# Turning the mLSTM's keys, values and heads by VectorE and DMA instead of TensorE; the norm's weight on the output gate

## The reference, cut to what matters

```python
s = jnp.einsum('bjhd,bshd->bhjs', q, k) * w                 # w: decay weights of a chunk
num = jnp.einsum('bhjs,bshe->bjhe', s, v) + inter * (q @ C)
h = num / jnp.maximum(jnp.abs(den), floor)
C_new = decay * C + jnp.einsum('bhs,bshd,bshe->bhde', w_last, k, v)
...
h = h * lax.rsqrt(jnp.mean(h * h, axis=-1, keepdims=True) + EPS)   # per head
h = (h.reshape(B, T, D_A) * p['mlstm_norm']).astype(x.dtype)
ya = (h * jax.nn.sigmoid(o)) @ p['w_proj_a']
```

## Time and profile before

| | |
|---|---|
| median of 3 runs | 1904.1 us (1902.83 to 1904.41) |
| span of the profiled execution | 1901.1 us |
| PE busy | 1881.8 us (99%) |
| DVE busy | 1348.0 us (71%) |
| ACT busy | 868.2 us (46%) |
| POOL busy | 110.5 us (6%) |
| DMA packets, bytes | 126553, 272.88 MB |

### The profile page before, as it was taken

The page is one execution under the profiler, slowest core; times in us unless marked ns, Lnnn a source line. Parts: engine busy times, 40 slices in busy tenths (PEclk is TensorE's granted clock), DMA queues, the critical chain, the costliest instruction groups (busy, mean ns, idle before and its releaser), DMA issues.

```text
span 1901.1 us, 33354 instructions
## 1 busy us (share of the span) xinstructions
PE 1881.8 (99%) x13291; PEld 1857.3 (98%) x13291; DVE 1348.0 (71%) x2082; ACT 868.2 (46%) x1629; POOL 110.5 (6%) x165
## 2 busy tenths in 40 slices
PE   9999999999999999999999999999999999999997
PEld 8999999999999999999999999999999999999997
DVE  7788999999987764784454378967777776746363
ACT  5554445444554455551122355644454444635342
POOL 0011111111111111110000000000000000000000
PEclk9999999999999999999999999999999999999999
DMA  3556676666657655458131333212222223556654
GB/s 135 160 142 151 163 186 162 165 184 172 188 171 199 195 157 155 145 157 338 45 139 45 119 100 104 81 69 79 81 81 69 77 83 113 183 202 210 208 172 160
DMA packets 126553, 272.88 MB, mean 144 GB/s; under 512 B 21820, under 2 KB 61500, under 8 KB 126400
## 3 DMA queue, kind: packets, MB, share of 16 engines
q1 hardware_dynamic: 111280, 235.16, 36.1%
q0 software_dynamic: 15120, 35.59, 10.3%
HBM read 206.97 MB, written 63.74 MB: 142 GB/s over the span
## 4 chain that ended last, share of the span: by engine, by line
PE 91%; DVE 4%; DMA 2%; issue 1%; ACT 1%; SPq 0%; POOL 0%; DVEq 0%; ACTq 0%; POOLq 0%
PE ps L1202 9%; PE ps L1204 9%; PE ps L1203 9%; PE ps L1367 7%; PE ps L1368 7%; PE ps L1369 7%; PE ps L1567 7%; PE ps L1565 7%; PE ps L1566 7%; PE ps L1587 4%; PE ps L1588 4%; PE ps L1589 4%; PE ps L1295 2%; PE ps L1292 1%; DMA araw<-wts 1%
## 5 line engine op out<-in xcount | busy, mean ns | idle before, releaser
L1202 PE MATMUL ps<-rx,fhi 128*128 128x364 f32 (+2 forms) x736 | 248.7, 338 | 0.1
L1203 PE MATMUL ps<-rx,fhi 128*128 128x364 f32 (+2 forms) x736 | 238.0, 323 | 0.0
L1204 PE MATMUL ps<-rx,flo 128*128 128x364 f32 (+2 forms) x736 | 238.0, 323 | 0.0
L1367 PE MATMUL ps<-rx,ahi 128*128 128x304 f32 (+1 forms) x672 | 194.4, 289 | 0.4 <-DVE v L2588 0.4
L1368 PE MATMUL ps<-rx,ahi 128*128 128x304 f32 (+1 forms) x672 | 193.7, 288 | 0.0
L1369 PE MATMUL ps<-rx,alo 128*128 128x304 f32 (+1 forms) x672 | 193.6, 288 | 0.0
L1587 PE MATMUL ps<-ghi,dhi 128*128 128x384 f32 (+1 forms) x528 | 173.2, 328 | 2.8 <-DVE glo L2949 2.0
L1588 PE MATMUL ps<-glo,dhi 128*128 128x384 f32 (+1 forms) x528 | 172.2, 326 | 0.0
L1589 PE MATMUL ps<-ghi,dlo 128*128 128x384 f32 (+1 forms) x528 | 172.2, 326 | 0.0
L2942 DVE TENSOR_TENSOR dlo<-draw,dhi 128x1408 fp32r<-128x1408 f32 x48 | 77.8, 1624 | 118.1 <-ACT dhi L2154 118.0
L1202 PEld LDWEIGHTS ps<-rx,fhi 128*128 128x128 f32 x736 | 138.6, 188 | 1.9 <-issue 0.3
(11 more groups left out here) (367 smaller groups left out, 5721.7 us busy)
## 6 DMA issues: line engine op xcount, KB each, us to landing
draw<-wdn SPq DMA_DIRECT2D x48, 704.0 KB, 4.2
araw<-wts SPq DMA_DIRECT2D x105, 256.0 KB, 3.9
uraw<-wts SPq DMA_DIRECT2D x44, 512.0 KB, 4.3
fraw<-wts SPq DMA_DIRECT2D x27, 512.0 KB, 3.8
qkv<-scr_qkv SPq DMA_DIRECT2D x22, 544.0 KB, 8.4
scr_g<-cva SPq DMA_DIRECT2D x22, 512.0 KB, 2.6
alo<-wts POOLq DMA_DIRECT2D x42, 256.0 KB, 5.1
graw<-scr_g SPq DMA_DIRECT2D x43, 192.0 KB, 4.1
```

Of the source, the lines that this page charges most:

```text
L1202: pe.matmul(b, hi[:, w], src[:, his[k], cols], start=(k == 0), stop=False)
L1203: pe.matmul(b, hi[:, w], src[:, los[k], cols], start=False, stop=False)
L1204: mm = pe.matmul(b, lo[:, w], src[:, his[k], cols], start=False, stop=(k == KB - 1))
L1367: pe.matmul(b, ahi[s][:, c], bhi[:, k, :], start=(fresh and k == 0), stop=False, skip_group_check=True)
```

## The change: what it does

- The keys and values are no longer turned by PE. SP loads the values of one chunk (`load_values`, three slots before the step) to `vin`; the keys stand in `qkv` as before, the value blocks of it are no longer loaded. DVE transposes squares of 32x32 inside both (`turn`, two slots before). SP stores the squares to a new DRAM tensor `scr_t` in such an order that the 128x128 blocks are turned (`store_turned`: four DMAs of 32 partitions each, in runs of 32 elements), and loads them back as `kvt`, keys and values side by side (`load_turned`, one DMA in rows of 128 elements). Before this load SP waits until the stores have landed and until ACT has weighted the keys of the step before.
- ACT weights the keys in place in SBUF (`weighted_keys`), one slot after the load; the copy of the values is gone.
- The head is turned by one DVE transpose of `zt` in squares (`rows_out`, DVE, two slots after the step); SP stores it in runs of 32 elements (`store_head`, four DMAs a step, two in the last chunk of each head).
- The norm's weight is put on the output gate: ACT makes mnq * tanh + mnq over the finished tile (one more operation of 1088 columns for each of the eight tiles, with a wait of SP's store on it), and `gated_head` is a plain product.
- `vin` and the two `turned` buffers lie where blocks 2 and 3 of head 0's `qkv` buffer were, so blocks 3 and 6 of the second pass change places (`C_HI`).

```diff
             def load_head(h):
...
-                for b in range(6):
+                for b in (0, 1, 4, 5):
                     sp.dma_start(qkv[h % 2][:, b, :], scr_qkv[h, b]).then_inc(qk_in, 16)
+            def load_values(i):
+                h, j = STEPS[i]
+                if i:
+                    sp.wait_ge(turned_set, 2 * i)
+                sp.dma_start(vin[:, :, :], scr_qkv[h, 2:4, :, step_cols(j)].rearrange("b p n -> p b n")).then_inc(v_part_in, 16)
+            def store_turned(i):
+                sp.wait_ge(turned_set, 2 * i + 2)
+                for a in range(4):
+                    rows = slice(32 * a, 32 * a + 32)
+                    sp.dma_start(scr_t[i][:, :, rows].rearrange("k (b n) q -> n (k b) q", n=32),
+                                 turned[i % 2][rows, :, :].rearrange("n k (b q) -> n (k b) q", q=32)).then_inc(turned_out, 16)
+            def load_turned(i):
+                if i >= 2:
+                    sp.wait_ge(n_full, i - 1)
+                if i:
+                    sp.wait_ge(kw_set, i)
+                sp.wait_ge(turned_out, 64 * (i + 1))
+                sp.dma_start(kvt[i % 2][:, 0:2 * DH]..., scr_t[i]...).then_inc(kvt_in, 16)
+            def store_head(i):
+                sp.wait_ge(zs_set, i + 1)
+                for b in Z_PARTS[i]:
+                    sp.dma_start(scr_z[2 * h:2 * h + 2, :, at + 32 * b:at + 32 * b + 32].rearrange("k (a q) n -> q (k a) n", q=32),
+                                 zs[i % 2][32 * b:32 * b + 32, :].rearrange("q (a n) -> q a n", n=32)).then_inc(z_out[i % 2], 16)
...
             for s, ((kind, k), c) in enumerate(SLOTS):          # SP
+                i = step_at(s, 0)   ->  load_turned(i)
+                i = step_at(s, -1)  ->  store_turned(i)
+                i = step_at(s, -3)  ->  load_values(i)
...
+                i = step_at(s, 3)   ->  store_head(i)
...
             def scores(i):                                       # PE
-                    pe.wait_ge(kv_copied, 2 * i)
-                for b in range(4):
-                    mm = pe.transpose(bank(2, b * P, P), q[:, b, cols], ident[:, :])
-            def rows_out(i):
-                for b in range(2):
-                    mm = pe.transpose(bank(3, 256 + b * L, L), zt[i % 2][:, b * P:(b + 1) * P], ident[:, :])
...
             def scores(i):                                       # ACT
-                act.activation(vt[p][:, 0:DH], bank(2, DH, DH), ACT.Copy).then_inc(kv_copied, 1)
-                act.activation(kw[p][:, :], bank(2, 0, DH), ACT.Copy, scale=gt[...])
+            def weighted_keys(i):                                # at step_at(s, 1), ahead of scores
+                act.wait_ge(kvt_in, 32 + 16 * (i + 1))
+                act.activation(kvt[p][:, 0:DH], kvt[p][:, 0:DH], ACT.Copy, scale=gt[...]).then_inc(kw_set, 1)
-                    act.activation(zs[p][:, b, :], bank(3, 256 + b * L, L), ACT.Copy, scale=mnq[...]).then_inc(zs_set, 1)
+                        act.activation(spl[i % 2][:, :], spl[i % 2][:, :], ACT.Identity, bias=mnq[:, k:k + 1], scale=mnq[:, k:k + 1])
...
+            def turn(i):                                         # DVE, at step_at(s, -2)
+                dve.wait_ge(turned_out, 64 * (i - 1))
+                dve.wait_ge(v_part_in, 32 + 16 * (i + 1))
+                dve.transpose(turned[p][:, 2:4, :], vin[:, :, :]).then_inc(turned_set, 1)
+                dve.transpose(turned[p][:, 0:2, :], qkv[h % 2][:, 0:2, step_cols(j)]).then_inc(turned_set, 1)
+            def rows_out(i):                                     # DVE, at step_at(s, 2), ahead of turn
+                dve.wait_ge(zt_set, i + 1)
+                dve.transpose(zs[p][:, :], zt[p][:, :]).then_inc(zs_set, 1)
...
-                dve.scalar_tensor_tensor(z, fx[:, n, :], 1.0, z, ALU.add, ALU.mult).then_inc(zo_set, 1)
+                dve.tensor_tensor(z, fx[:, n, :], z, ALU.mult).then_inc(zo_set, 1)
```

More of the change, by code:

```diff
@@ L94 @@
 SPL_OF = {"u": (0, 2), "g": (1, 2), "k": (1, 1), "v": (0, 0), "q": (0, 0)}
-SPL_AT = [1 + sum(sum(SPL_OF[kind]) for kind, _ in PAIRS_B[:i]) for i in range(NB + 1)]
+SPL_AT = [2 + sum(sum(SPL_OF[kind]) for kind, _ in PAIRS_B[:i]) for i in range(NB + 1)]
 V0_STORES = [[1 - p + len(range(p, min(i, NB), 2)) for i in range(NB + 2)] for p in range(2)]
@@ L203, in step_at, with z_stored @@
     return STEP_IN.get(NTH_FULL[s] - after)
[L206 to L213, removed]
+Z_PARTS = [range(L // 32) if j < NCHUNK else range((L - DEC) // 32, L // 32) for _, j in STEPS]
+def z_stored(i):
+    return 16 * sum(len(Z_PARTS[n]) for n in range(i % 2, i, 2))
 def step_cols(j):
@@ L463, in build @@
     qkv = [Room(at_rz + s * 6 * blk)(f"qkv{s}", [P, 6, T]) for s in range(2)]
+    room = Room(at_rz + 2 * blk)
+    vin = room("vin", [P, 2, L])
+    turned = [room(f"turned{s}", [P, 4, L]) for s in range(2)]
+    assert room.at <= at_rz + 4 * blk
     room = Room(at_rz + 6 * blk)
@@ L479, in build @@
     cb = [room(f"cb{s}", [P, 2, VW]) for s in range(2)]
-    vt = [room(f"vt{s}", [P, VW]) for s in range(2)]
-    kw = [room(f"kw{s}", [P, DH]) for s in range(2)]
+    kvt = [room(f"kvt{s}", [P, DH + VW]) for s in range(2)]
     wt = [room(f"wt{s}", [P, L]) for s in range(2)]
@@ L484, in build @@
     zt = [room(f"zt{s}", [P, DH]) for s in range(2)]
-    zs = [room(f"zs{s}", [P, 2, L]) for s in range(2)]
+    zs = [room(f"zs{s}", [P, DH]) for s in range(2)]
     nb = [room(f"nb{s}", [P, L]) for s in range(2)]
@@ L640, in build @@
         zt_set = sem("zt_set")
-        z_full = sem("z_full")
         zs_set = sem("zs_set")
@@ L861, in _ @@
             for s, ((kind, k), c) in enumerate(SLOTS):
+                i = step_at(s, 0)
+                if i is not None:
+                    load_turned(i)
+                i = step_at(s, -1)
+                if i is not None:
+                    store_turned(i)
+                i = step_at(s, -3)
+                if i is not None:
+                    load_values(i)
                 i = step_at(s, 1)
@@ L923, in _ @@
                     sp.dma_start(c_out[0][:, STEPS[i][0]], cb[0][:, :, :]).then_inc(cp_out, 16)
+                i = step_at(s, 3)
+                if i is not None:
+                    store_head(i)
                 i = step_at(s, 4)
@@ L1423, in _ @@
                     gate_turn()
-                i = step_at(s, 3)
-                if i is not None:
-                    rows_out(i)
                 i = step_at(s, 1)
@@ L1747, in evac @@
                         act.activation(spl[i % 2][:, :], spl[i % 2][:, :], ACT.Copy, bias=0.5, scale=0.5).then_inc(spl_set, 1)
+                    if kind == "o" and c == NC - 1:
+                        act.wait_ge(t_free, EVAC_AT[s])
+                        act.activation(spl[i % 2][:, :], spl[i % 2][:, :], ACT.Identity, bias=mnq[:, k:k + 1], scale=mnq[:, k:k + 1])\
+                            .then_inc(spl_set, 1)
                 elif kind == "mu":
@@ L1881, in _ @@
                     a_hi(0, 5), a_hi(0, 6), a_hi(0, 2), a_hi(0, 7), a_hi(0, 4), a_minus(0, 2), a_minus(0, 4)
+                i = step_at(s, 1)
+                if i is not None:
+                    weighted_keys(i)
                 i = step_at(s, 0)
@@ L2660, in _ @@
                     gate_columns()
+                i = step_at(s, 2)
+                if i is not None:
+                    rows_out(i)
+                i = step_at(s, -2)
+                if i is not None:
+                    turn(i)
                 i = step_at(s, 0)
```

88 lines of the change are left out of this document (42 added, 46 removed).

## The result

The changed kernel takes 1983.9 us (median of 4, 1982.3 to 1986.2), the kernel before 1903.8 us on the same chip: ratio 1.0422 (95% interval 1.0410 to 1.0435). It is 80 us slower. I forecast 1926 us with a range of 1886 to 1972: the sign was right, the size was not.

What follows compares the result with a forecast made beforehand. The prediction took the DMA engines' work to bound the steps: 292 us plus 6 us for SP's order gives 298 instead of 276, so 1901.1 + 22 + 3 = 1926 us, range 1886 to 1972.

Steps and rivals of the forecast that it cites:

- What bounds it: Stretch of all steps: PE bounds before, busy 99%; DVE and DMA get its work, and DMA was thought to decide.
- the gate: ACT's extra operation of 1.10 us on each of eight output gate tiles: costed at nothing, up to 1 us.
- TensorE, -0.65 us a step: PE loses four transposes (0.43 us) and the head's two (0.22 us) a step: 23.4 us over 36 steps.
- VectorE, 0.33 us a transpose, step of 6.6 us: DVE gains three transposes, 1.0 us a step; at 6.6 us it just keeps PE's new pace in the tap steps.
- The packets' price, 12.2 ns: Time of one 128-byte packet on one DMA engine, from a line through the 120-byte and 256-byte prices.
- rival 3: Scattered 128-byte writes cost about 24 ns, twice the small bursts' price: 1986 us, chance 0.15.
- DMA's work, 268 us, and a step of 8.1 us: DMA work in the steps' stretch rises from 160 to 268 us; with `nb`'s pauses a step takes 8.1 us, 36 make 292.
- `nb`'s quiet part: Load of `nb` occupies SP's queue 1.5 us a step, each engine busy a tenth of the time; later transfers wait.
- SP's order: SP issues 4.4 of 6.6 us a step, keeping pace if stores land under 4.35 us; later heads' blocks add 6 us.
- a share under 0.8: Sign in the profile after: late PE steps with DMA share under 0.8 mean the order of SP's list is the cause.
- a share over 0.9: Sign for the forecast in the profile after: DMA share over 0.9 in the steps' stretch, with steps 8.1 us apart.

Runs made afterwards that it cites:

- 1904.8 with nothing turned: Changed kernel without the keys' and values' DMA trip and VectorE transposes (ScalarE copies them unturned), head stored early in one transfer: 1904.8 us.
- the run where ScalarE stores and nobody reads: Changed kernel, ScalarE copies replacing the keys' and values' reload, head stored early in one transfer; ScalarE issues their four 128-byte-packet stores, read by nobody: 1932.6 us.
- the kernel with ScalarE's stores: Changed kernel with the head's store one slot earlier and the four stores of turned keys and values issued by ScalarE one slot earlier: 1939.3 us.
- 1976.4: Changed kernel with the head's store and the stores of turned keys and values each one slot earlier, all issued by SP: 1976.4 us.

## Why the prediction was right and wrong

The forecast was a stretch 22 us longer; it became 79 us longer, 16.7 before the first step and 62.7 in the steps. Put in a row, differences between runs come near the whole: 1904.8 with nothing turned, + 9.8 for VectorE's transposes, + 40.0 for the keys' and values' store, + 33.0 for the head's store narrow and late, gives 1987.6 against 1983.9 measured. This does not show that the reload and the serial trip cost nothing. The 40.0 us were measured with the stores in another place than the changed kernel has them, the 33.0 us with two alterations at once and without the trip, while the head's early store gives back only 20 in the changed kernel. That the sum fits may be luck.

- **What bounds it.** Right in that the loss lies with VectorE and DMA, which got the work, and that the gate costs nothing (1903.5 us). Wrong in what of DMA it is: not the engines' work, but issuing and landing in SP's queue.
- **TensorE, -0.65 us a step.** Right for the head's 0.22 us, which the head part alone gives back in full. For the 0.43 us of keys and values it is not shown.
- **VectorE, 0.33 us a transpose, step of 6.6 us.** Right in size: in the changed kernel they take 0.40 us and start 0.33 to 0.37 us apart, the undisturbed step is 6.72 us (634.61 to 641.33 for the same operation). What I did not draw from it: at 6.6 for TensorE and 6.7 for VectorE there is next to no slack to make up for a delay.

```profile
634.61 0.43 DVE L2430 TENSOR_TENSOR hn<-ps,hn 128x257 f32<-128x257 f32 x1
...
641.33 0.42 DVE L2430 TENSOR_TENSOR hn<-ps,hn 128x257 f32<-128x257 f32 x1
```

- **The packets' price, 12.2 ns.** Right. In the run where ScalarE stores and nobody reads (1932.6 us), its queue holds these packets alone, from 574 to 850 us:

```profile
q10 hardware_dynamic: 71808, 8.92, 20.1%
```

  0.201 x 276 x 16 / 71808 = 12.4 ns. So rival 3's time, 1986 us, came out by another cause. The Trainium skill (DMA: Bandwidth & Descriptors, Specifications) speaks of a read-modify-write under 512 bytes; no doubling is seen in this price.
- **DMA's work, 268 us, and a step of 8.1 us.** The work was 0.80 x 356 = 285 us, 6% more. A step of 8.0 us and a share of 0.92 are what the kernel with ScalarE's stores has, 1939 us, inside my own range of 1908 to 1950. The term fits that kernel, which may be luck: no run shows that the engines' work is what holds it, and its ScalarE stands 37.7 us at issuing. One row I misread: the slices of 1 and 2 in the earlier trace rows last from 606.5 to 607.6 us, so `nb`'s quiet part is 1.1 us and not 1.5, which takes up to 0.4 us off the 8.1.
- **SP's order: "So SP's loop and the engines' work say the same."** This is the step that failed. I priced SP at 4.4 us of 6.6 and asked only when the stores of `turned` land (under 4.35 us). They do in the median, 3.2 us; the longest took 12.3, and those that last 5 us or more can stand in the chain, as the 8.46 us above. The rows after (ns min/median/max):

```profile
L824 SPq DMA_DIRECT2D scr_t<-turned x144: 303/536/3612, 574.2 to 898.7; - x144
...
DMA to landing us min/median/max: 2.1/3.2/12.3
```
```profile
L818 SPq DMA_DIRECT2D vin<-scr_qkv x36: 376/530/4685, 539.3 to 880.2; - x36
```
```profile
L841 SPq DMA_DIRECT2D scr_z<-zs x136: 302/451/2253, 614.1 to 926.1; - x136
```

  A store of 512 packets takes 0.54 us to issue where I had 0.44, so a step's ten transfers and `nb` take 4 x 0.54 + 4 x 0.45 + 0.38 + 0.53 + 0.48 = 5.4 us. More than that, an issue takes up to 4.7 us when the queue is held up, and the earlier trace rows had shown the like (2807 ns for `fx`), of which I made nothing. And I followed one trip only. The loads and stores that stand behind the stores in the list, values and heads, have VectorE waiting for them. For SP's order I had added 6 us in all; taking the four stores of keys and values off SP, and nothing else, gives back 37 (from 1976.4 to 1939.3). With the big stores out of SP's list and the head's issued a slot earlier, 45 of the 80 us are back.
- My own last test, a share under 0.8 for "the order of SP's list is the cause", was a poor one: the share was 0.80 to 0.82, and a large part of the loss came by SP all the same. The other signs I named for the forecast, a step of 8.1 us and a share over 0.9, did not come: 9.2 us and 0.82.
- **Not foreseen: TensorE's clock.** 1.00 in all of the stretch before, 0.92 after, so it was at 1.2 instead of 2.4 GHz for some 2 x 0.08 x 356 = 57 us, which can cost at most 28. It falls after TensorE stood idle: four matmuls that take 1.03 us before take 2.05 here, behind a wait of 3.06 us, in a stretch whose granted clock is 0.50 (second row, third number from the end).

```profile
627.38 2.05 PE L1333 MATMUL ps<-cb,qkv 128*128 128x257 f32 x4 [3.06 <-ACT kvt L1705]
```
```profile
628.00:630.00 2.00, 2.00 (x6) 1.63 (x5) 0.00 (x0) 0.00 (x0) 0.00 (x0) 0.50 0.67 100
```

  No run separates its cost from that of the waits.

## What to carry to other kernels

Price a DMA twice: what it takes of the 16 engines, and what it takes of the list that issues it, with everything that stands behind it in that list. When two engines' lists are both full, look for the load that a full engine waits for and let another queue carry the bulk; and of a change with two parts, try each alone: here the head part alone is 0.4% faster than the kernel before, and the keys' and values' part alone loses eight times that (63 us).

## What was not expected of the hardware

- Issue time on SP's queue isn't a constant: 0.30 us at least, 0.54 in the median and 3.6 at most for 512 packets of 128 bytes; the longest of a 128 KB load was 4.7 us, while POOL's queue had the engines (a share of 1.02 from 585 to 590 us, SP's queue 0.17).
- From ScalarE's queue (the run of 1932.6 us) the same stores took 0.51 us in the median and 6.1 at most, and ScalarE's own work stood still meanwhile.

```profile
L1693 ACTq DMA_DIRECT2D scr_t<-turned x144: 309/510/6123, 576.4 to 862.5; - x144
```

- VectorE's transpose of 128x256 four-byte elements takes 0.40 us (0.45 behind an operation on another tile or a wait), as long as a plain operation on one tile of this size.
